# A chunk inverse on TensorE, VectorE and ScalarE, before and after its growth levels run over 32 of 64 columns

## The chip, the cores and the metric

One core of a Trainium2 chip runs the whole program in one launch. The metric is the device time of that launch in microseconds (us), the median of three runs.

## What is computed

The program is a chain of four layers on 1024 tokens of width 1024, in float32. The change lies in the second one, a RWKV-7 time mixing with 16 heads of 64. Each head carries a 64x64 state through the tokens:

```
def step(state, inp):
    r_t, w_t, k_t, v_t, al_t, be_t = inp
    sa = jnp.einsum("bhvk,bhk->bhv", state, al_t)
    state = (state * w_t[:, :, None, :] + sa[..., None] * be_t[:, :, None, :]
             + v_t[..., None] * k_t[:, :, None, :])
    return state, jnp.einsum("bhvk,bhk->bhv", state, r_t)
```

Taken in chunks of 64 tokens, the steps of a chunk are coupled by `sa`: token t needs the updates of all earlier tokens of its chunk. That coupling is a strictly triangular 64x64 matrix for each head and chunk, and all of the chunk's updates together are (identity minus that matrix) inverted, times a right side. So the kernel inverts 16 heads x 16 chunks of unit triangular 64x64 matrices.

## The kernel before

The function is `rwkv_chunks`. Two heads lie above one another on the 128 partitions (rows 0 to 63 and 64 to 127), eight such pairs `j` side by side; a group `g` is four pairs. Every 64x64 product of the stage is a float32 matmul for one head, which the trace shows as two MATMUL records and two LDWEIGHTS records; a "step" over one group is 4 pairs x 2 heads = 8 products = 16 records.

The inverse is grown block by block. `N` holds the coupling matrix, `T` the inverse so far and `Tt` its transpose. Both start as the identity (GpSimd, `start_t`); `products` on VectorE (DVE) fills the 2x2 blocks. Then for each of five levels, lv = 0 to 4, blocks of b = 2, 4, 8, 16, 32 columns are joined in twos to blocks of 2b:

- `y_step` (TensorE, L1915): Y = product of `N` (weights) and `Tt` (moving), 16 records for each group, into PSUM banks 0 and 1.
- `take_y` (ScalarE, L2077): copies Y of each group, 4 pairs x 64 columns, to SBUF.
- `z_step` (TensorE): with weights `T` and moving `Y` (L1927), and, at levels 0 to 3, with weights `Y` and moving `T` (L1931); 16 records each for each group, into banks 2 and 3.
- `grow` (DVE): two masked copies for each group, PSUM into `Tt` (L2257) and at levels 0 to 3 into `T` (L2261). The mask `tmask` lets only the new off-diagonal blocks through.

Everything is over all 64 columns, though a level's new block lies, in `Tt`, only in the second half of each 2b columns, and in `T` only in the first half.

The order of the work is written out by hand, one stream for each engine, and engines wait for each other on semaphores. For chunk c's inverse and the finish of chunk c-1 TensorE runs: first products (L1879, L1885, L1892), right sides (L1941, L1942), a bonus product (L1898), solutions (L1953), y(0), the state update (L1961, L1962), z(0), outputs of group 0, y(1), outputs of group 1 (L1968 to L1970), z(1), a turn of `b` (L1904), y(2), a turn of `v`, z(2), y(3), a turn of `k`, z(3), the variance product (L1976), y(4), z(4). So most steps of the inverse have other products between them; z(2) to y(3), and y(4) to z(4), have none. Between first products of neighbouring chunks nothing but this list stands. SyncE loads the next chunk but one (1792 KB) in the meantime.

`Y` lies in a part of an SBUF tensor that the trace calls `u`, as `N` does; so `psum<-Tt_rc,u` is y_step, `psum<-u,T_rc` is L1927 and `u<-psum` at L2077 is the copy of Y.

Of the kernel before, what the change touches and what calls it, by code (L numbers as in the profile page):

```python
# [17 lines left out]
P = 128  # L18
# [1359 lines left out]
RW_C = 64  # L1378
# [402 lines left out]
def rwkv_chunks(nc, K, A, chunk, next_round, ahead):  # L1781

    J = KT
    GJ = J // 2
    LEVELS = (1, 2, 4, 8, 16, 32)
    NL = len(LEVELS) - 1
    T_STEPS, P_STEPS = 2 * (NL + 1), 2 * NL
    with nc.cleanup_on_exit(), ExitStack() as c:
        sb = lambda n, s, d=F32: c.enter_context(nc.sbuf_tensor(f"{n}_rc", s, d))
        sem = lambda n: nc.alloc_semaphore(f"{n}_rc")  # L1790
# [4 lines left out]
        G, dist, distx, E1, E2, E3, rhs, U, N, Y, bv, hn = (spare[:, n] for n in range(12))  # L1795
# [20 lines left out]
        n_ready, ak_ready, bv_ready = sem("n_ready"), sem("ak_ready"), sem("bv_ready")  # L1816
        turned = {n: sem(f"{n}_turned") for n in "bkv"}
        taken = {n: sem(f"{n}_taken") for n in "bkv"}
        y_done, y_ready, z_done, t_ready, plain_ready = (
            sem("y_done"), sem("y_ready"), sem("z_done"), sem("t_ready"), sem("plain_ready"))  # L1820
        rhs_done, rhs_ready, u_done, u_ready = sem("rhs_done"), sem("rhs_ready"), sem("u_done"), sem("u_ready")
# [5 lines left out]
        pairs = lambda n: K.bank_pair(n).rearrange("p (j a t) -> p j a t", j=J, a=2)  # L1827
        half = lambda n, h: K.psum[:, n, h * GJ * RW_C:(h + 1) * GJ * RW_C].rearrange("p (j t) -> p j t", j=GJ)
        flat = lambda x: x.rearrange("p j t -> p (j t)")
        cols = lambda name: K.par[:, COL[name]:COL[name] + J].rearrange("p (j a) -> p j a", a=1).broadcast_to(  # L1830
            [P, J, RW_C])
        Y_BANK, Z_BANK, N_BANK, BONUS, RHS, OUT = 0, 2, 4, 5, 6, 7
# [12 lines left out]
        with nc.Block() as block:  # L1845
# [26 lines left out]
            def _(pe):  # L1872
# [35 lines left out]
                def y_step(c, q, lv):  # L1908

                    for g in range(2):  # L1910
                        pe.wait_ge(t_ready, c * T_STEPS + (2 * lv + g + 1))
                        if lv == 0 and g == 0:
                            pe.wait_ge(n_ready, c + 1)
                        for j, hp in heads(g):
                            last = pe.matmul(half(Y_BANK + g, 0)[hp, j % GJ], N[hp, j, :], Tt[hp, q, j, :],  # L1915
                                             start=True, stop=True)
                        last.then_inc(y_done, 1)

                def z_step(c, q, lv):

                    for g in range(2):
                        if lv == 0 and g == 0:
                            pe.wait_ge(ak_ready, c + 1)
                        pe.wait_ge(plain_ready, c * P_STEPS + (2 * lv + g + 1))
                        pe.wait_ge(y_ready, c * P_STEPS + (2 * lv + g + 1))
                        for j, hp in heads(g):
                            last = pe.matmul(half(Z_BANK + g, 0)[hp, j % GJ], T[hp, q, j, :], Y[hp, j, :],  # L1927
                                             start=True, stop=True)
                        if lv < NL - 1:
                            for j, hp in heads(g):  # L1930
                                last = pe.matmul(half(Z_BANK + g, 1)[hp, j % GJ], Y[hp, j, :], T[hp, q, j, :],  # L1931
                                                 start=True, stop=True)
                        last.then_inc(z_done, 1)

                def right_sides(ch, p):
# [103 lines left out]
            @block.scalar  # L2039
            def _(act):  # L2040
                act.preload_act_table_set("natural_log_exp_and_others")

                def exponentials(n, p):
                    if n > 0:
                        act.wait_ge(ar_ready, n)
                        act.wait_ge(bk_ready, n)
                    act.wait_ge(d_ready, n + 1)
                    act.activation(E2, dist, ACT.Exp, scale=RW_DECAY)
                    act.activation(E1, dist, ACT.Exp, scale=-RW_DECAY).then_inc(e12_ready, 1)
                    act.activation(E3, distx, ACT.Exp, scale=-RW_DECAY).then_inc(e3_ready, 1)  # L2050
                    act.activation(em[:, p, :], G[:, :, RW_C // 2 - 1], ACT.Exp, scale=-RW_DECAY)
                    act.activation(ee[:, p, :], dist[:, :, RW_C - 1], ACT.Exp,
                                   scale=-RW_DECAY).then_inc(em_ready, 1)

                def squares(ch):
                    act.drain()
                    act.activation(sq[:, :, :], O[:, :, :], ACT.Square).then_inc(sq_ready, 1)

                def group_rstd(ch):
                    act.wait_ge(var_done, ch + 1)  # L2060
                    act.activation(flat(rs[:, :, :]), K.psum[:, VAR, :], ACT.Ln, scale=1.0 / RW_C,
                                   bias=gn_eps[:, 0:1])
                    act.drain()
                    act.activation(rs[:, :, :], rs[:, :, :], ACT.Exp, scale=-0.5).then_inc(rs_ready, 1)

                def high_part(ch):
                    act.wait_ge(out_ready, ch + 1)
                    act.mul(K.m_hi[:, 0:J, slice(ch * RW_C, ch * RW_C + RW_C)], O[:, :, :], U_SCALE).then_inc(hi_ready, 1)

                def take(done, ready, x, b, ch):  # L2070
                    act.wait_ge(done, ch + 1)
                    act.copy(x, bank(b)).then_inc(ready, 1)

                def take_y(c, lv):
                    for g in range(2):
                        act.wait_ge(y_done, c * P_STEPS + (2 * lv + g + 1))
                        act.copy(Y[:, g * GJ:g * GJ + GJ], half(Y_BANK + g, 0)).then_inc(y_ready, 1)  # L2077

                def take_turned(c, n, x):
                    act.wait_ge(turned[n], c + 1)  # L2080
                    act.copy(x, bank(TURN[n])).then_inc(taken[n], 1)

                def body(ch, p, inverse, finish, following):
                    c, q = ch + 1, 1 - p
                    if inverse:
                        act.wait_ge(n_done, c + 1)
                        act.copy(N, bank(N_BANK)).then_inc(n_ready, 1)
                    if finish:
                        take(rhs_done, rhs_ready, rhs, RHS, ch)
                        take(u_done, u_ready, U, OUT, ch)  # L2090
                    if inverse:
                        take_y(c, 0)
                    if finish and ch > 0:
                        high_part(ch - 1)
                        act.wait_ge(lo_ready, ch)
                    if inverse:
                        take_y(c, 1)
                    if finish:
                        act.wait_ge(o_done, ch + 1)
                        act.copy(O[:, :, :], bank(OUT)).then_inc(o_ready, 1)  # L2100
                    if inverse:
                        take_turned(c, "b", bT[:, q])
                        take_y(c, 2)
                        take_turned(c, "v", vT[:, q])
                    if following:
                        exponentials(ch + 2, p)
                    if inverse:
                        take_y(c, 3)
                    if finish:
                        squares(ch)  # L2110
                    if inverse:
                        take_turned(c, "k", kT[:, q])
                        take_y(c, 4)
                    if finish:
                        group_rstd(ch)

                exponentials(0, 0)
                act.wait_ge(t_init, 1)
                chunk_steps(body)
                high_part(RW_N - 1)  # L2120
# [62 lines left out]
            def _(dve):  # L2183
# [4 lines left out]
                dve.drain()  # L2188
                dve.scalar_tensor_tensor(centre[:, :], K.pair_ones[:, :], -1.0 / RW_C, K.ident[:, :],
                                         ALU.mult, ALU.add).then_inc(centre_ready, 1)  # L2190
                dve.sem_inc(h_ready, 1)

                def summed(n, p):
# [60 lines left out]
                def grow_turned(lv, g, q, data):  # L2254

                    mask = tmask[:, 0, lv:lv + 1, :].broadcast_to([P, GJ, RW_C])
                    dve.copy_predicated(Tt[:, q, g * GJ:g * GJ + GJ], mask, data).then_inc(t_ready, 1)  # L2257

                def grow_plain(lv, g, q, data):
                    mask = tmask[:, 1, lv:lv + 1, :].broadcast_to([P, GJ, RW_C])  # L2260
                    dve.copy_predicated(T[:, q, g * GJ:g * GJ + GJ], mask, data).then_inc(plain_ready, 1)  # L2261

                def grow(c, q, lv):
                    for g in range(2):
                        dve.wait_ge(z_done, c * P_STEPS + (2 * lv + g + 1))
                        grow_turned(lv + 1, g, q, half(Z_BANK + g, 0))
                        if lv + 1 < NL:
                            grow_plain(lv + 1, g, q, half(Z_BANK + g, 1))

                def body(ch, p, inverse, finish, following):  # L2270
                    c, q, n = ch + 1, 1 - p, ch + 2
# [1106 lines left out]
```

## Time and profile before

| | |
|---|---|
| median of three runs | 3453.41 us (3447.71, 3453.41, 3459.82) |
| the profiled execution | 3451.49 us |
| its span, first to last instruction | 3449.7 us |
| PE busy (matmul records) | 3276.7 us, 95% of the span |
| DVE, ACT, POOL busy | 54%, 41%, 13% |
| mean granted TensorE clock | 0.981 |

PE is TensorE's matmul stream, PEld its weight loads, DVE is VectorE, ACT is ScalarE, POOL is GpSimd. A MATMUL record runs from its start until its result is out, so neighbouring records overlap; how fast the engine gets through them is seen from the starts, not from the durations. "Idle before, releaser" names what ended a gap; "issue" is a gap that nothing in the profile explains. The chunk stage runs from 1331 to 1850 us.

### The profile page before, as it was taken

The page shows a single profiled execution, that of the slowest core. Times are in us where ns is not written, and L with a number is a line of the kernel's source. Part 1 is how long each engine was busy: PE and PEld are TensorE (multiplying, and loading weights), DVE is VectorE, ACT ScalarE, POOL GpSimd, SP SyncE. Part 2 cuts the span into 40 slices and gives each one's busy share as a digit, 9 for nine tenths or more (in the row PEclk, how much of TensorE's full clock was granted, in tenths as well). Part 3 has the DMA queues.
Part 4 walks back from the last instruction along what each step waited for, and adds up shares of the span by engine and source line. Part 5 has one row for each costly group of instructions (what it writes and reads, how often), then busy time and mean ns, then how long its engine had stood idle before and what let it go on. Part 6 is the DMA issues. An engine that isn't in the chain of part 4 may idle for free. (4 is left out here: it accounts for less than half of the span.)

```text
span 3449.7 us, 73665 instructions
## 1 busy us (share of the span) xinstructions
PE 3276.7 (95%) x32618; PEld 2033.5 (59%) x32618; DVE 1852.2 (54%) x2557; ACT 1423.0 (41%) x2045; POOL 436.3 (13%) x302
## 2 busy tenths in 40 slices
PE   6999999999899797999999899999999999999999
PEld 3446565644444346999886466657644466657544
DVE  4666767662526524666553566654453366754342
ACT  3554545433655422333333445542322255533321
POOL 3000000020000002334331132300000232200000
PEclk9999999999999998999999999999999999999999
DMA  5111111130355552111112111021021211020211
GB/s 177 37 49 46 39 39 34 43 118 17 98 127 123 123 139 77 68 68 56 58 46 87 55 32 54 7 60 32 17 91 49 68 43 37 1 66 26 65 67 49
DMA packets 308210, 214.84 MB, mean 62 GB/s; under 512 B 125403, under 2 KB 283950, under 8 KB 305326
## 3 DMA queue, kind: packets, MB, share of 16 engines
q1 hardware_dynamic: 307464, 210.18, 20.4%
q8 instruction: 236, 3.87, 0.5%
q10 hardware_dynamic: 458, 0.37, 0.0%
q14 instruction: 52, 0.43, 0.0%
HBM read 172.74 MB, written 41.98 MB: 62 GB/s over the span
## 5 line engine op out<-in xcount | busy, mean ns | idle before, releaser
L142 PE MATMUL psum<-u,w_hi 128*128 128x512 f16 x1856 | 555.5, 381 | 17.3 <-PEq L197 5.4
L142 PE MATMUL psum<-u,w_lo 128*128 128x512 f16 x928 | 353.3, 381 | 0.0
L142 PEld LDWEIGHTS psum<-u,w_hi 128*128 128x128 f16 x1856 | 181.4, 98 | 245.8 <-issue 23.0
L115 DVE SCALAR_TENSOR_TENSOR w_lo<-stage,w_hi 128x1024 f16<-128x1024 f32 x140 | 170.4, 1238 | 217.1 <-ACT w_hi L109 216.5
L174 PE MATMUL psum<-u,w_hi 128*128 128x512 f16 x896 | 271.4, 381 | 0.0
L2650 DVE CUSTOM_DVE_ANT_0 probs_att<-psum,bias_att 128x1024 f32<-128x1024 f32 x128 | 156.8, 1225 | 165.4 <-PE psum L2445 165.0
L1071 PE MATMUL psum<-w_hi,merged 128*128 128x512 f16 x768 | 233.4, 382 | 6.8 <-PEq L3072 4.5
L2423 PE MATMUL psum<-u,w_hi 128*128 128x512 f16 x768 | 232.2, 384 | 6.7 <-PEq L1109 6.7
L1071 PE MATMUL psum<-held_hi_out,merged 128*128 128x512 f16 x768 | 231.2, 379 | 0.0
L97 POOL TENSOR_TENSOR w_hi<-stage,w_scale 128x1024 f16<-128x1024 f32 x36 | 69.1, 1920 | 946.6 <-PE psum L2423 839.3
L190 PE MATMUL psum<-w_hi,u 128*128 128x128 f16 x2048 | 173.2, 219 | 0.0
L190 PE MATMUL psum<-w_lo,u 128*128 128x128 f16 x1024 | 172.4, 219 | 0.0
L174 PE MATMUL psum<-u,w_lo 128*128 128x512 f16 x448 | 170.0, 379 | 0.0
L109 ACT ACTIVATE w_hi<-stage 128x1024 f16<-128x1024 f32 x140 | 144.7, 1050 | 55.0 <-DMA stage<-w_in 32.2
L2257 DVE COPY_PREDICATED Tt_rc<-tmask_rc,psum 128x256 f32<-128x256 uint32 x192 | 83.6, 444 | 145.1 <-PE psum L1931 121.3
L190 PEld LDWEIGHTS psum<-w_hi,u 128*128 128x128 f16 x2048 | 157.9, 98 | 4.9 <-issue 4.6
L142 PE MATMUL psum<-mix_b_rp,w_hi 128*128 128x512 f16 x480 | 145.2, 385 | 13.7 <-ACT work_rp L1681 12.7
L142 PEld LDWEIGHTS psum<-u,w_lo 128*128 128x128 f16 x928 | 91.0, 98 | 110.9 <-issue 2.1
L2559 ACT ACTIVATE probs_att<-probs_att,neg_max_att 128x1024 f32<-128x1024 f32 x128 | 146.3, 1146 | 16.2 <-DVE neg_max_att L2654 16.2
L2473 PEld LDWEIGHTS psum<-turned_att,merged 128*128 128x128 f32 x1024 | 132.6, 193 | 28.6 <-issue 14.6
L2473 PE MATMUL psum<-turned_att,merged 128*128 128x128 f32 x1024 | 138.0, 278 | 11.4 <-ACT sq_att L2573 11.0
L2423 PE MATMUL psum<-u,w_lo 128*128 128x512 f16 x384 | 147.3, 384 | 0.0
(463 smaller groups left out, 6987.6 us busy)
## 6 DMA issues: line engine op xcount, KB each, us to landing
stage<-w_in SPq DMA_DIRECT2D x72, 512.0 KB, 5.0
X<-rwkv_chunks SPq DMA_DIRECT2D x14, 1792.0 KB, 8.1
stage<-ab_w_in SPq DMA_DIRECT2D x48, 512.0 KB, 4.8
stage<-rw_w_in SPq DMA_DIRECT2D x32, 512.0 KB, 4.7
rwkv_chunks<-work_rp SPq DMA_DIRECT2D x26, 512.0 KB, 5.9
stage<-w_out SPq DMA_DIRECT2D x24, 512.0 KB, 4.2
X<-x SPq DMA_DIRECT2D x16, 512.0 KB, 8.5
stage<-ab_w_out SPq DMA_DIRECT2D x16, 512.0 KB, 4.7
```

Source lines behind the costliest of these rows:

```text
L97: pool.tensor_tensor(K.w_hi[:, slot, :], K.stage[:, slot, :], scale, ALU.mult).then_inc(K.w_half[slot], 1)
L109: act.mul(K.w_hi[:, slot, :], K.stage[:, slot, :], W_SCALE).then_inc(K.w_half[slot], 1)
L115: dve.scalar_tensor_tensor(K.w_lo[:, slot, :], K.stage[:, slot, :], W_SCALE, K.w_hi[:, slot, :], ALU.mult, ALU.subtract).then_inc(K.w_full ...
L142: last = pe.matmul(K.psum[:, bank, :], w[:, k, :], u[:, k, cols], start=(k == 0 and n == 0), stop=(k == KT - 1 and n == 2))
L174: last = pe.matmul(K.psum[:, banks[half], :], w[:, k, :], u[:, k, half * HALF:(half + 1) * HALF], start=(k == 0 and n == 0), stop=(k == KT ...
L190: last = pe.matmul(out, u[:, k, toks], w[:, k, :], start=(k == 0 and n == 0), stop=(k == KT - 1 and n == 2))
L1071: last = pe.matmul(out, m[:, 2 * u + k, t * P:(t + 1) * P], w[:, at, w_cols], start=(u == 0 and k == 0 and n == 0), stop=(u == UH - 1 and ...
L2257: dve.copy_predicated(Tt[:, q, g * GJ:g * GJ + GJ], mask, data).then_inc(t_ready, 1)
L2423: last = pe.matmul(K.psum[:, PROJ + half, :], w[:, kt, :], u[:, kt, cols(half)], start=(kt == 0 and n == 0), stop=(kt == KT - 1 and n == 2))
L2473: last = pe.matmul(K.psum[:, O_BANK, (i % 4) * P:(i % 4 + 1) * P], v_tiles[h % 2][:, half * 4 + n, :], turned[:, half, n, :], start=(half ...
L2559: act.activation(probs[:, s % 2, m, :], probs[:, s % 2, m, :], ACT.Exp, bias=neg_max[:, s % 2, m:m + 1], accum_out=sums[:, s % 2, m:m + 1] ...
L2650: dve.tensor_tensor_reduce(probs[:, s % 2, m, :], K.bank_pair(m), bias[:, h % 2, at:at + S], LOGIT_UNSCALE, LOWEST, ALU.add, ALU.max, neg_ ...
```

## The change

Two helpers choose, for level lv, the half n (0 or 1) of every 2b columns, with b = `LEVELS[lv + 1]` = 2, 4, 8, 16, 32: a view of 32 columns in runs of b. y_step and L1927 stream and write only half 1, the second product of z_step (L1931) only half 0; the copy of Y and the masked copies take the same halves. Weights stay whole (64 columns); since `Y` as weights is read whole and its other half is no longer written at level 0, `Y` is set to zero once. The number of instructions stays as it was but for that memset and its semaphore.

```diff
+        def side(x, lv, n):
+            b = LEVELS[lv + 1]
+            if len(x.shape) == 2:
+                return x.rearrange("p (n a b) -> p n a b", a=2, b=b)[:, :, n, :]
+            return x.rearrange("p j (n a b) -> p j n a b", a=2, b=b)[:, :, :, n, :]
+
+        def side_mask(n, lv):
+            b = LEVELS[lv + 1]
+            m = side(tmask[:, n, lv + 1:lv + 2, :], lv, 1 - n)
+            return m.broadcast_to([P, GJ, RW_C // (2 * b), b])
...
-                            last = pe.matmul(half(Y_BANK + g, 0)[hp, j % GJ], N[hp, j, :], Tt[hp, q, j, :],
-                                             start=True, stop=True)
+                            last = pe.matmul(side(half(Y_BANK + g, 0)[hp, j % GJ], lv, 1), N[hp, j, :],
+                                             side(Tt[hp, q, j, :], lv, 1), start=True, stop=True)
...
-                            last = pe.matmul(half(Z_BANK + g, 0)[hp, j % GJ], T[hp, q, j, :], Y[hp, j, :],
-                                             start=True, stop=True)
+                            last = pe.matmul(side(half(Z_BANK + g, 0)[hp, j % GJ], lv, 1), T[hp, q, j, :],
+                                             side(Y[hp, j, :], lv, 1), start=True, stop=True)
...
-                                last = pe.matmul(half(Z_BANK + g, 1)[hp, j % GJ], Y[hp, j, :], T[hp, q, j, :],
-                                                 start=True, stop=True)
+                                last = pe.matmul(side(half(Z_BANK + g, 1)[hp, j % GJ], lv, 0), Y[hp, j, :],
+                                                 side(T[hp, q, j, :], lv, 0), start=True, stop=True)
...
                 def take_y(c, lv):
+                    if c == 0 and lv == 0:
+                        act.wait_ge(y_zeroed, 1)
...
-                        act.copy(Y[:, g * GJ:g * GJ + GJ], half(Y_BANK + g, 0)).then_inc(y_ready, 1)
+                        act.copy(side(Y[:, g * GJ:g * GJ + GJ], lv, 1),
+                                 side(half(Y_BANK + g, 0), lv, 1)).then_inc(y_ready, 1)
...
+                dve.memset(Y, 0.0).then_inc(y_zeroed, 1)
                 dve.sem_inc(h_ready, 1)
...
-                        grow_turned(lv + 1, g, q, half(Z_BANK + g, 0))
+                        dve.copy_predicated(side(Tt[:, q, group], lv, 1), side_mask(0, lv),
+                                            side(half(Z_BANK + g, 0), lv, 1)).then_inc(t_ready, 1)
...
-                                grow_plain(lv + 1, g, q, half(Z_BANK + g, 1))
+                                dve.copy_predicated(side(T[:, q, group], lv, 0), side_mask(1, lv),
+                                                    side(half(Z_BANK + g, 1), lv, 0)).then_inc(plain_ready, 1)
```

## Rows read from the trace of the kernel before

**Rows 1.** Busy time in four stretches: length, then busy and records, clock, DMA.

```profile
core 0: us, PE busy (x) PEld busy (x) DVE busy (x) ACT busy (x) POOL busy (x), PEclk, DMA share, GB/s
1348.00:1660.00 312.00, 304.52 (x8826) 285.58 (x8823) 190.19 (x342) 112.23 (x253) 118.38 (x109) 0.99 0.18 63
```

**Rows 2.** Timeline of PE, late in a chunk: start, length from first start to last end.

```profile
1448.88 1.44 PE L1915 MATMUL psum<-Tt_rc,u 64*64 64x64 f32 x30
1450.15 1.10 PE L1904 MATMUL psum<-ident,kt_rc 64*64 64x64 f32 x32
1451.08 0.63 PE L1927 MATMUL psum<-u,T_rc 64*64 64x64 f32 x16
1451.55 0.63 PE L1931 MATMUL psum<-T_rc,u 64*64 64x64 f32 x16
...
1453.04 1.13 PE L1976 MATMUL psum<-sq_rc,pair_ones 128*128 128x512 f32 x2
1454.10 1.15 PE L1915 MATMUL psum<-Tt_rc,u 64*64 64x64 f32 x32
1455.35 1.05 PE L1927 MATMUL psum<-u,T_rc 64*64 64x64 f32 x29
```

**Rows 3.** Groups of the chunk stage on PE and PEld, shapes kept apart.

```profile
L1927 PE MATMUL psum<-u,T_rc 64*64 64x64 f32 x2560 | 114.8, 223 | 6.1 <-issue 4.2 <-ACT u L2077 0.6
L1915 PE MATMUL psum<-Tt_rc,u 64*64 64x64 f32 x2560 | 103.5, 224 | 2.2 <-issue 0.9
L1931 PE MATMUL psum<-T_rc,u 64*64 64x64 f32 x2048 | 94.0, 219 | 9.4 <-issue 9.4
L1915 PEld LDWEIGHTS psum<-Tt_rc,u 64*64 64x64 f32 x2560 | 93.0, 139 | 18.0 <-DVE Tt_rc L2257 15.0 <-issue 3.0
```

**Rows 4.** Timeline of PE, first products of another chunk.

```profile
1551.75 1.13 PE L1885 MATMUL psum<-bt_rc,ar_rc 64*64 64x64 f32 x32
1552.68 1.95 PE L1892 MATMUL psum<-ar_rc,kt_rc 64*64 64x128 f32 x32
1554.43 0.33 PE L1941 MATMUL psum<-vT_rc,ak_rc 64*64 64x64 f32 x4
```

**Rows 5.** Timeline of another stage, L716: 64 weight columns, 32 or 64 moving columns.

```profile
639.79 1.01 PEld L716 LDWEIGHTS psum<-qe_hg,ke_hg 128*64 128x64 f32 x32 [0.48 <-DVE qe_hg L954]
639.79 1.13 PE L716 MATMUL psum<-qe_hg,ke_hg 128*64 128x32 f32 x32 [0.34 <-DVE qe_hg L954]
658.92 1.02 PEld L716 LDWEIGHTS psum<-qe_hg,ke_hg 128*64 128x64 f32 x32 [0.54 <-issue]
658.93 1.15 PE L716 MATMUL psum<-qe_hg,ke_hg 128*64 128x64 f32 x32
```

**Rows 6.** Groups on DVE and ACT by shape.

```profile
L2257 DVE COPY_PREDICATED Tt_rc<-tmask_rc,psum 128x256 f32<-128x256 uint32 x192 | 83.6, 444 | 145.1 <-PE psum L1931 121.3 <-PE psum L1927 23.4
L2261 DVE COPY_PREDICATED T_rc<-tmask_rc,u 128x256 f32<-128x256 uint32 x32 | 32.5, 1067 | 3.5 <-ACT u L2087 3.5
L968 DVE COPY_PREDICATED st_hg<-room,psum 128x512 f32<-128x512 uint32 x32 | 23.3, 727 | 2.1 <-issue 2.1
L2077 ACT COPY u<-psum 128x256 f32<-128x256 f32 x160 | 59.7, 373 | 159.2 <-PE psum L1915 155.2
L2072 ACT COPY u<-psum 128x512 f32<-128x512 f32 x32 | 18.7, 585 | 72.0 <-PE psum L1942 47.3 <-PE psum L1953 24.7
```

**Rows 7.** Timelines of DVE and ACT around z(2) and y(4) of the chunk of rows 2.

```profile
1448.20 0.45 DVE L2257 COPY_PREDICATED Tt_rc<-tmask_rc,psum 128x256 f32<-128x256 uint32 x1 [1.41 <-PE psum L1931]
1448.54 0.43 DVE L2261 COPY_PREDICATED T_rc<-tmask_rc,psum 128x256 f32<-128x256 uint32 x1
1449.13 0.45 DVE L2257 COPY_PREDICATED Tt_rc<-tmask_rc,psum 128x256 f32<-128x256 uint32 x1 [0.16 <-PE psum L1931]
...
1454.83 0.84 ACT L2077 COPY u<-psum 128x256 f32<-128x256 f32 x2 [2.91 <-PE psum L1915]
```

**Rows 8.** Timelines of DVE and PE where the stage begins.

```profile
1321.29 0.48 DVE L2187 MEMSET Hs_rc<- 128x512 f32 x1
1321.86 0.29 DVE L2189 SCALAR_TENSOR_TENSOR centre_rc<-pair_ones,ident 128x128 f32<-128x128 f32 x1
1322.07 1.63 DVE L2197 TENSOR_TENSOR_SCAN u<-reset_rc,X 128x512 f32<-128x512 f32 x1
...
1331.55 3.68 PE L1879 MATMUL psum<-ar_rc,bt_rc 64*64 64x128 f32 x32 [15.56 <-DVE ar_rc L2211]
```

**Rows 9.** A pause of PE, then busy time in two stretches of 8 us.

```profile
1356.93 0.50 PE L1931 MATMUL psum<-T_rc,u 64*64 64x64 f32 x10 [2.06 <-issue]
...
1349.00:1357.00 8.00, 5.87 (x194) 5.65 (x192) 2.78 (x7) 3.66 (x9) 3.54 (x3) 1.00 0.66 231
1357.00:1365.00 8.00, 7.93 (x163) 7.79 (x164) 4.66 (x11) 1.33 (x3) 0.00 (x0) 0.79 0.02 4
```

More of the change, by code:

```diff
@@ L1818, in rwkv_chunks @@
         taken = {n: sem(f"{n}_taken") for n in "bkv"}
+        y_zeroed = sem("y_zeroed")
         y_done, y_ready, z_done, t_ready, plain_ready = (
@@ L2265, in grow @@
                         dve.wait_ge(z_done, c * P_STEPS + (2 * lv + g + 1))
-                        grow_turned(lv + 1, g, q, half(Z_BANK + g, 0))
+                        group = slice(g * GJ, g * GJ + GJ)
+                        dve.copy_predicated(side(Tt[:, q, group], lv, 1), side_mask(0, lv),
+                                            side(half(Z_BANK + g, 0), lv, 1)).then_inc(t_ready, 1)
                         if lv + 1 < NL:
-                            grow_plain(lv + 1, g, q, half(Z_BANK + g, 1))
+                            dve.copy_predicated(side(T[:, q, group], lv, 0), side_mask(1, lv),
+                                                side(half(Z_BANK + g, 1), lv, 0)).then_inc(plain_ready, 1)
                 def body(ch, p, inverse, finish, following):
```

## The prediction

> **What bounds the kernel now.** I read the busy time by stretches first, to see which engine the chunk stage leaves no room. Over 312 us of it PE is busy 304.5, DVE 190, ACT 112 [rows 1]. The busy share of a pipelined engine says little, so the timeline of PE comes next, and there the starts. A step of 32 records starts at 1450.15 and the next one at 1451.08: 0.93 us, 29.1 ns a record; 16 records take 0.47 us, the same pace [rows 2]. Nearly every step of a chunk runs at this pace, whatever its line. What departs from it is small. The last 30 records of y(3) need 1.27 us, from 1448.88 to 1450.15, where the pace gives 0.87: 0.40 beyond. z(4) starts 1.25 us after y(4), where it gives 0.93: 0.32 beyond [rows 2]. So the stage is PE's own pace, plus two waits of 0.7 us together in a chunk of 31, plus pauses without a releaser [rows 9]. The question is therefore what sets 29.1 ns, and whether 32 moving columns in place of 64 lower it.
>
> **The matmul records: y_step and z_step.** The change touches 2560 + 2560 + 2048 = 7168 records [rows 3]. Their moving columns go from 64 to 32, their weight loads stay 64x64, one for each record.
>
> What does the pace follow? With 64 weight columns and 128 moving ones, 32 records take 1.75 us, 54.7 ns each; with 64 moving ones 0.93 us, 29.1 ns [rows 4]. From 128 to 64 the moving columns set the pace. From 64 to 32 another stage of this kernel answers: it has float32 weights of 64 columns, in two tiles of the array in turn, as the two heads are here, and moves 32 or 64 columns. With 32 moving columns, 32 records last 1.13 us from first start to last end; less one record of 0.22 that is 0.91 over 31, 29.3 ns. With 64 it is 1.15, so 30 ns. The weight loads are equally far apart in both, (1.01 - 0.14)/31 = 28 ns, by a load of 0.14 [rows 5]. So the pace with 32 columns is that with 64: the loads of 64 weight columns, which the change leaves, take the place of the moving columns. I take 0 ns for each record. The difference of the two rows, 0.6 ns, times 7168 would be 4 us; I leave it in the range.
>
> The tiles there lie beside one another in columns, here above one another in rows, so the two bounds are wide. Below: if weight loads did not hold it, halving the moving columns would halve the pace as from 128 to 64, by 13 to 15 ns a record, 93 to 105 us. Above: what strided runs cost, for which no row here exists; all matmul rows of the profile that I found write contiguous columns. Per moving column the engine may become twice as slow before it shows, since 32 columns then take what 64 take. The price beyond that is a rival, below.
>
> The Trainium skill (TensorE: Matmul & The Clock Gate, section "Wait — 56ns, not 53.3ns?") puts a floor of about 25 ns between starts however few columns move. By that floor alone the sum would be an estimated 7168 x 4.1 ns = 29 us shorter, with the weight loads it is not; the rows on 32 moving columns stay above that floor [rows 5].
>
> **The masked copies (L2257, L2261).** 444 ns for 256 columns, 727 ns for 512 of the same operation with its data in PSUM [rows 6]: 1.1 ns a column, so 128 columns take about 303 ns, 141 less, if runs of 2 to 32 columns go at the same rate. Bounds: 0 less, if short runs cost twice as much each; and more than now, if the operation fell to the rate of its form with all operands in SBUF, 1067 ns for 256, thus 530 for 128, 90 more [rows 6]. I take 303, the nearest in form. DVE is not what bounds the stage, so this counts only where PE waits: at y(3). There z(2) of group 1 ends, DVE starts at 1449.13 (it was idle before, so no earlier copy delays it), and PE may go on about 0.44 later [rows 7]. The other levels have 0.9 us or more of other products between z and y. So 0.14 x 16 chunks = 2.3 us. The wait of 0.40 shrinks and does not close, so nothing else is late in its place.
>
> **The copy of Y (L2077).** 373 ns for 256 columns, 585 for 512: 0.83 a column, 267 ns for 128, 106 less [rows 6]. Bounds as above, 0 less to 106 less; a rate twice as slow for short runs gives 0. It counts at z(4), where PE waits for group 0's copy, started at 1454.83 [rows 7]. In 13 of the 16 chunks PE waits there; in the other three a delay just before hides it. 0.106 x 13 = 1.4 us. At the other levels the copy is under the state update, the outputs or a turn.
>
> **Chunk 0** has nothing of a former chunk in between, so its z(0) and y(1) wait as well: 0.1 + 0.14 = 0.25 us.
>
> **The memset of Y.** The one like it takes 0.48 us and with the step to the next instruction 0.57 [rows 8]. It stands ahead of the scan at L2197 on DVE; behind that are the distances, ACT's exponentials and `ar`, for which PE's first product waits 15.56 us [rows 8]. Nothing hides it: +0.57 us. ACT's new wait for it is met 19 us earlier than Y is first copied; nothing is held up behind it.
>
> **The sum.** -2.3 - 1.4 - 0.25 + 0.57 = -3.4 us. Against the profiled execution, 3451.5 us (span 3449.7 plus 1.8 around it), that is 3448.1. This execution lies 1.9 under the median of the runs, so for the median I put 3453.4 - 3.4 = 3450.0. What can be told from no change here is about 0.3%, 10 us; the three runs before lie 12 apart.
>
> **The rivals.**
>
> *Pace follows the moving columns.* For it: 128 to 64 did, and the tiles here are rows of the array, not columns. Against it: the weight loads alone are 28 ns apart with 32 moving columns [rows 5]. Time: 448 touched records in each of 16 chunks at 13.3 ns less are 95 us. A faster PE meets DVE and ACT earlier: z(2) of group 1 would take 0.25 us in place of 0.47, less than the two masked copies of group 0 ahead of it on DVE (0.6), so y(3) waits some 0.2 longer in each chunk, 3 us. With the 3.4 of the other terms: 3453.4 - 95 + 3 - 3 = about 3358. Half way there, 3405, also belongs here. Chance 0.11.
>
> *Strided runs slow the matmul.* The place: level 0, where the runs are 2 columns (8 bytes) with gaps of 2, and if the shape of the runs matters more, levels 1 to 3 too; at level 4 the 32 columns are contiguous. It decides from the point where a moving column costs more than twice what it costs now. If level 0's 96 records in a chunk took 58 in place of 29 ns: 96 x 16 x 29 = 45 us, 3493; if it were only a third slower, 15 us, 3463. For it the trace has nothing; against it stands the slack of two. Chance 0.12. The Trainium skill (Advanced Engine Details and Errata, section "PSUM Cachelines") speaks for it: any non-contiguous pattern slows matmuls significantly, though it asks only for every two elements in a row for best throughput, which runs of 2 still are. No row here shows either.
>
> *The pauses move.* PE stands in some chunks in the middle of z(3) with no releaser, in rows 9 for 2.06 us, while 0.66 of the DMA engines are taken, and in the stretch behind one of them the granted clock is 0.79, that is 1.2 GHz for a part of it [rows 9]. Which chunks are hit may shift with a chunk that is 0.25 us shorter. One more or less is worth 2.1 us and, at 0.21 of 8 us, 1.7 behind it: about 4 us. Two more make 3458, no change; three, 3462, or more end slower. Chance 0.07.
>
> *The forecast.* PE's pace stays, two waits shrink. Chance 0.70.
>
> **How the numbers follow.** Forecast 3450, own range 3443 to 3459, from the spread of the runs, the bounds of the copies (0 to 3.7 us of gain, or 2 us of loss) and one pause. 8 in 10 must take in the nearer parts of the rivals, so 3430 to 3466. Faster by over 0.3%: 0.11 of the first rival and 0.06 of the forecast, 0.17. Slower: 0.08 of strided runs, 0.04 of pauses, 0.02 of the forecast, 0.14. Within 0.3%: 0.69.
>
> **What would show it.** After: y and z records with 32 moving columns, still 0.47 us for 16 of them and weight loads of 0.14 at the same distances; L2257 near 303 ns, L2077 near 267; the hole in y(3) near 0.15 and z(4) 1.15 behind y(4); a chunk's period some 0.25 shorter; one more memset of 0.48 before the scan. It is wrong if 16 records of level 4 take clearly less than 0.47 us (weight loads don't hold the pace), if 16 of level 0 take clearly more (strides cost), or if the sum of the pauses changes by more than the rest.

## The result, and the profile after

| | before | after |
|---|---|---|
| median of 20 runs each | 3450.07 us (3440.65 to 3459.82) | 3467.62 us (3449.51 to 3478.62) |
| ratio, 95% interval | | 1.0053 (1.0041 to 1.0065) |
| profiled execution, its span | 3451.49, 3449.7 us | 3470.7, 3468.9 us |
| mean granted TensorE clock | 0.981 | 0.975 |
| chunk stage, first to last matmul | 525.1 us | 545.8 us |

The change makes the kernel 0.5% slower, about 18 us. The forecast was 3450 and its range ended at 3466, so it was wrong. The two profiled executions differ by 19.2 us, and the chunk stage alone by 20.7; what comes before it is about 1 us shorter. The engines after, from the first part of the profile's page:

```profile
PE 3295.3 (95%) x32618; PEld 2052.7 (59%) x32618; DVE 1812.2 (52%) x2558; ACT 1407.9 (41%) x2045; POOL 435.7 (13%) x302
```

DVE and ACT lost work (before 1852.2 and 1423.0). PE gained 18.6 us with as many records of fewer columns. The groups of the chunk stage say where (columns as in [rows 3, 6]):

```profile
L1942 PE MATMUL psum<-u,T_rc 64*64 64x32 f32 x2560 | 115.8, 224 | 9.1 <-issue 7.8 <-ACT u L2094 1.4
L1930 PE MATMUL psum<-Tt_rc,u 64*64 64x32 f32 x2560 | 102.7, 225 | 1.4 <-issue 1.4
L1946 PE MATMUL psum<-T_rc,u 64*64 64x32 f32 x2048 | 95.2, 221 | 8.2 <-issue 8.2
L2286 DVE COPY_PREDICATED Tt_rc<-tmask_rc,psum 128x128 f32<-128x128 uint32 x160 | 52.3, 327 | 183.9 <-PE psum L1946 144.5 <-PE psum L1942 39.4
L1894 PE MATMUL psum<-ar_rc,bt_rc 64*64 64x128 f32 x512 | 45.1, 345 | 15.6 <-DVE ar_rc L2230 15.6
...
L2094 ACT COPY u<-psum 128x128 f32<-128x128 f32 x160 | 42.9, 269 | 175.2 <-PE psum L1930 171.1
```

L1942, L1930 and L1946 are the narrowed products; their means are within 2 ns of those of [rows 3]. The line that grew is one that the change does not touch. L1894 is the first products, L1879 before, where its row was:

```profile
L1879 PE MATMUL psum<-ar_rc,bt_rc 64*64 64x128 f32 x512 | 33.4, 282 | 15.6 <-DVE ar_rc L2211 15.6
```

It went from 282 to 345 ns. In each chunk these products come right behind z(4). An undisturbed chunk does what the forecast said. PE's timeline late in such a chunk after the change, the stretch of [rows 2] one chunk on:

```profile
1490.34 1.26 PE L1930 MATMUL psum<-Tt_rc,u 64*64 64x32 f32 x30
1491.44 1.13 PE L1919 MATMUL psum<-ident,kt_rc 64*64 64x64 f32 x32
1492.40 0.61 PE L1942 MATMUL psum<-u,T_rc 64*64 64x32 f32 x16
1492.84 0.63 PE L1946 MATMUL psum<-T_rc,u 64*64 64x32 f32 x16
...
1495.39 1.12 PE L1930 MATMUL psum<-Tt_rc,u 64*64 64x32 f32 x32
1496.50 1.12 PE L1942 MATMUL psum<-u,T_rc 64*64 64x32 f32 x32
```

The starts of the two steps shown are 0.44 us apart, against 0.47 before; the pairs behind them stay at 0.47. y(3) lasts 1.10 from start to start where it took 1.27, z(4) starts 1.11 behind y(4) where it took 1.25 [rows 2]. The chunk's period falls from 30.95 to 30.61 us.

The loss lies behind the pauses. A pause is here a gap of over 1.2 us between the starts of neighbouring records of PE. One after the change, in z(3) of another chunk, on PE's timeline, and the busy time (columns as in [rows 1]) in stretches cut along it:

```profile
1424.34 0.63 PE L1946 MATMUL psum<-T_rc,u 64*64 64x32 f32 x16
1427.45 0.95 PE L1942 MATMUL psum<-u,T_rc 64*64 64x32 f32 x16 [2.48 <-issue]
...
1429.18 2.07 PE L1991 MATMUL psum<-sq_rc,pair_ones 128*128 128x512 f32 x2
1431.19 1.92 PE L1930 MATMUL psum<-Tt_rc,u 64*64 64x32 f32 x32
1432.92 1.90 PE L1942 MATMUL psum<-u,T_rc 64*64 64x32 f32 x32
1434.62 3.52 PE L1894 MATMUL psum<-ar_rc,bt_rc 64*64 64x128 f32 x32
1437.98 1.09 PE L1900 MATMUL psum<-bt_rc,ar_rc 64*64 64x64 f32 x32
...
1424.00:1428.00 4.00, 1.52 (x49) 1.44 (x45) 0.49 (x2) 0.70 (x2) 0.48 (x1) 0.95 0.61 255
1428.00:1431.00 3.00, 3.00 (x26) 1.62 (x23) 1.69 (x4) 0.00 (x0) 0.00 (x0) 0.50 0.02 5
1431.00:1434.60 3.60, 3.60 (x65) 3.41 (x66) 0.30 (x1) 1.64 (x4) 0.00 (x0) 0.50 0.00 0
1434.60:1437.80 3.20, 3.20 (x35) 3.20 (x34) 0.99 (x2) 0.11 (x1) 1.63 (x2) 0.50 0.02 5
1437.80:1440.00 2.20, 2.20 (x58) 2.20 (x56) 1.64 (x4) 0.59 (x1) 1.94 (x2) 0.98 0.00 0
```

The granted clock is 0.50 (1.2 GHz) from the end of the pause to the last of the first products (L1894), 10.2 us. The 32 first products take 3.36 us from start to start; before, behind such a pause, they took 1.75. Here is one of those, from the timeline and the busy time of the kernel before:

```profile
1742.39 0.45 PE L1927 MATMUL psum<-u,T_rc 64*64 64x64 f32 x9 [2.00 <-issue]
...
1743.24 1.57 PE L1976 MATMUL psum<-sq_rc,pair_ones 128*128 128x512 f32 x2
1744.74 1.98 PE L1915 MATMUL psum<-Tt_rc,u 64*64 64x64 f32 x32
1746.50 1.46 PE L1927 MATMUL psum<-u,T_rc 64*64 64x64 f32 x32
1747.76 1.95 PE L1879 MATMUL psum<-ar_rc,bt_rc 64*64 64x128 f32 x32
1749.51 1.13 PE L1885 MATMUL psum<-bt_rc,ar_rc 64*64 64x64 f32 x32
...
1743.80:1747.20 3.40, 3.40 (x48) 2.46 (x48) 1.52 (x4) 0.81 (x3) 0.00 (x0) 0.50 0.00 0
1747.20:1754.00 6.80, 6.80 (x183) 6.80 (x180) 5.68 (x9) 1.74 (x3) 3.59 (x3) 1.00 0.01 2
```

A like pause, with the same steps behind it, but the clock is back after 3.4 us, while z(4) runs. Over the stage there were six pauses (14.5 us together) before and five stretches at 1.2 GHz of 3.4 us, 17.0 us. After, there were eight pauses (17.6 us), of which seven last 2.0 to 2.7 us and one 1.2; behind the seven lie one low stretch of 6.8 us and six of 10.2, 68.0 us. The low clock at the start of the stage, which ends during chunk 0's first products in all runs, is left out of these sums. The 51 us more at half the clock are worth up to 25.5 us. With 3.1 us more of pauses, and 16 x 0.34 = 5.4 less by shorter waits, that makes up to 23; the stage grew by 20.7. The other executions agree: the mean granted clock is 0.973 to 0.978 in all 20 of the kernel after, and 0.979 to 0.986 in the 29 of the kernel before that ran beside the first four experiments.

### The profile page after: what moved, and what is told of

It reads as the page before. It is cut to its first block and busy times, and to the rows that moved or that the text cites. A ratio compares the mean times of both kernels' runs of the same rounds, so it can differ in the third digit from the quotient of the medians.

```text
span 3468.9 us, 73667 instructions
## 1 busy us (share of the span) xinstructions
PE 3295.3 (95%) x32618; PEld 2052.7 (59%) x32618; DVE 1812.2 (52%) x2558; ACT 1407.9 (41%) x2045; POOL 435.7 (13%) x302
## 5 line engine op out<-in xcount | busy, mean ns | idle before, releaser
L2495 PEld LDWEIGHTS psum<-turned_att,merged 128*128 128x128 f32 x1024 | 131.7, 191 | 28.6 <-issue 14.5
L2286 DVE COPY_PREDICATED Tt_rc<-tmask_rc,psum 128x128 f32<-128x128 uint32 x160 | 52.3, 327 | 183.9 <-PE psum L1946 144.5
```

What stands on the lines that cost most here:

```text
L2286: dve.copy_predicated(side(Tt[:, q, group], lv, 1), side_mask(0, lv), side(half(Z_BANK + g, 0), lv, 1)).then_inc(t_ready, 1)
L2495: last = pe.matmul(K.psum[:, O_BANK, (i % 4) * P:(i % 4 + 1) * P], v_tiles[h % 2][:, half * 4 + n, :], turned[:, half, n, :], start=(half ...
```

## The experiments

The ratio is always that to the kernel before, run in the same batch. "Low" is the time at 1.2 GHz within the stage in the one profiled execution, that at the start of the stage left out.

**Matmuls alone.** The change, with the copy of Y and both masked copies over 64 columns again.

```diff
-                        act.copy(side(Y[:, g * GJ:g * GJ + GJ], lv, 1),
-                                 side(half(Y_BANK + g, 0), lv, 1)).then_inc(y_ready, 1)
+                        act.copy(Y[:, g * GJ:g * GJ + GJ], half(Y_BANK + g, 0)).then_inc(y_ready, 1)
...
+                        grow_turned(lv + 1, g, q, half(Z_BANK + g, 0))
...
+                            grow_plain(lv + 1, g, q, half(Z_BANK + g, 1))
```

> Only the matmuls run over 32 columns; the copy of Y and the masked copies are those of before, over 64. Theory A: the loss comes from the 32-column products alone, through the clock: after a pause in z(3) the clock stays at 1.2 GHz some 10 us in place of 3.4, so seven chunks of 35 to 38 us, L1894 (first products) at a mean near 345 ns in place of 282; without the 0.25 us a chunk that the copies give back, 1.006 to 1.008 of before (3471 to 3478). Rival B: the narrower copies shift the stages and so the pauses; then this kernel is before's time, 3450, within 5. Rival C: strides cost TensorE time: then 16 records take over 0.47 us at level 0.

3473.05 against 3447.62 us, ratio 1.0066 (1.0047 to 1.0085). Low 71.4 us. Of this, 6.8 us lie in chunk 0 and 3.4 in a later chunk, with no pause over 1.2 us before them. The whole loss is there without any shorter copy, so the rival that the copies shift something falls. Behind the pause at 1724 the busy time shows the clock as after the change:

```profile
1728.00:1737.00 9.00, 9.00 (x128) 8.18 (x128) 3.50 (x8) 1.96 (x4) 2.90 (x3) 0.52 0.01 2
1737.00:1739.00 2.00, 2.00 (x47) 2.00 (x45) 1.12 (x4) 0.59 (x1) 0.68 (x1) 1.00 0.00 0
```

**Copies alone.** The other half: matmuls over 64 columns, copies over 32.

```diff
-                            last = pe.matmul(side(half(Y_BANK + g, 0)[hp, j % GJ], lv, 1), N[hp, j, :],
-                                             side(Tt[hp, q, j, :], lv, 1), start=True, stop=True)
+                            last = pe.matmul(half(Y_BANK + g, 0)[hp, j % GJ], N[hp, j, :], Tt[hp, q, j, :],
+                                             start=True, stop=True)
```

And so for both products of z_step.

> Only the copy of Y and the masked copies run over 32 columns; the matmuls are those of before. Theory A: the gain that the prediction summed, 3 to 6 us, and low stretches as short as before: 0.9985, near 3446. Rival B (the shift of the stages is what costs): near 3467, 1.005.

3445.64 us, 0.9997 (0.9985 to 1.0008). Low 17.0 us, as before. The profiled stage is 3.3 us shorter, but the gain does not stand out of the spread of the runs.

**The last level wide.** The change, with y(4) and z(4) over 64 columns; levels 0 to 3 stay narrow.

```diff
+                            if lv < NL - 1:
                                 last = pe.matmul(side(half(Y_BANK + g, 0)[hp, j % GJ], lv, 1), N[hp, j, :],
                                                  side(Tt[hp, q, j, :], lv, 1), start=True, stop=True)
+                            else:
+                                last = pe.matmul(half(Y_BANK + g, 0)[hp, j % GJ], N[hp, j, :], Tt[hp, q, j, :],
+                                                 start=True, stop=True)
...
```

> The kernel after, but y(4) and z(4), the products that run behind the pause and the variance product, are over 64 columns again; levels 0 to 3 stay at 32. Theory A: those two steps are what TensorE does when the clock is low, so it comes back as soon as before: 3445 to 3450, 0.999. Rival D (the columns of all levels count, because the clock falls by what went before): 3460 to 3468, long low stretches.

3446.53 us, 0.9992 (0.9981 to 1.0004): the loss is gone. The pauses are not gone: eight, 19.1 us. Six of the seven low stretches are 3.4 us long, one 6.8, in all 27.2. Busy time behind one pause, cut where the clock comes back:

```profile
1424.00:1427.40 3.40, 3.40 (x56) 2.87 (x56) 1.10 (x2) 1.11 (x3) 0.00 (x0) 0.52 0.00 0
1427.40:1434.00 6.60, 6.60 (x173) 6.60 (x171) 5.36 (x9) 1.23 (x3) 3.59 (x3) 0.99 0.01 2
```

So whether these 64 records a chunk, between the pause and the first products, move 32 or 64 columns decides most of the length.

**The last level alone narrow.** The kernel before, with only the matmuls of y(4) and z(4) over 32 columns (the condition of the last diff turned round, all copies wide).

> The kernel before (all copies over 64 columns), but the matmuls of y(4) and z(4) over 32. Theory A: nearly the whole loss comes back with a third of the narrow products gone: 1.004 to 1.007, long low stretches (L1894-like first products near 340 ns in the mean). Rival D: 0 to a third of it, 3450 to 3457.

3457.74 us, 1.0024 (1.0010 to 1.0039), low 47.7 us. This is a loss, but under the bound expected. In the profiled execution the low stretches are 6.8, 10.2, 3.4, 10.2, 3.4 and 13.7 us: behind some pauses the clock returns early even with narrow y(4) and z(4). That execution took 3467.12 us, close to the slowest of the twelve, so a usual one probably has less low clock; the mean granted clock of the twelve runs from 0.976 to 0.984. The last level is needed for the loss; that it suffices for all of it is not shown. What the narrow products of the other levels add is left open.

**No burst of DMA.** The pauses fall together with SyncE's load of the next chunk but one (1792 KB in one DMA, 0.61 of the DMA engines in the stretch above). Here each load brings 32 KB; the chunk stage's inputs are left out but for these. Once with the kernel before, once with the change.

```diff
-                    sp.dma_start(raw[:, p], A["scratch"][ch]
-                                 ).then_inc(raw_in[p], 16)
+                    sp.dma_start(raw[:, p, G_, 0:1], A["scratch"][ch, :, G_, 0:1]).then_inc(raw_in[p], 16)
```

> The kernel before, but each of the 14 loads of a chunk's inputs (1792 KB) brings only one pair's gate, 32 KB; the rest of the chunk's inputs stays that of the first two chunks, so the output leaves this out. If the pauses of TensorE in z(3) come with the load, none over 1.2 us is left and no low clock after the first products of chunk 0: 14.5 us of pauses, 8.5 of low clock and the small delays go, some 25 to 28 us: 3420 to 3425, 0.9925. If they come from elsewhere: 3447.

> The same edit on the kernel after (the same inputs left out). Theory A: with no pause there is no low clock to stay in, and what the prediction summed is left: 3 to 6 us less than the kernel before with small loads, so 3416 to 3421, 0.991 of before; periods of a chunk 30.6 us throughout. Rival E (narrow products are slower to run at this place in themselves, or lower the clock without a pause): 15 us or more over before with small loads, near 3440.

Before so: 3429.20 against 3448.45, 0.9938 (0.9922 to 0.9955), a little above the 3420 to 3425 expected. After so: 3420.61, 0.9920 (0.9901 to 0.9938). Neither profiled execution has a pause or a low stretch, and the order of the two turns round: the narrow kernel's median is 8.6 us the lower. The intervals overlap; in the profiled executions the stage takes 495.5 us against 500.4, 4.9 less, within the 3 to 6 expected. Busy time over the stretch of [rows 1], first the narrow one, then the wide one:

```profile
1348.00:1660.00 312.00, 312.00 (x9236) 295.45 (x9232) 177.45 (x356) 109.02 (x269) 120.85 (x111) 1.00 0.02 5
```

```profile
1348.00:1660.00 312.00, 310.21 (x9112) 291.78 (x9110) 195.14 (x352) 117.07 (x265) 120.48 (x110) 1.00 0.02 5
```

124 records more in 312 us without a change of clock: that is the gain of the change by itself.

**The load in pieces.** The whole load, as seven DMAs of 256 KB, each behind a step of the former chunk.

```diff
-            eng.wait_ge(raw_in[p], ch * 8 + (16 - 8 * p))
+            eng.wait_ge(raw_in[p], (ch - p) * 8 * RW_ARRAYS + 16)
...
-                    sp.dma_start(raw[:, p], A["scratch"][ch]
-                                 ).then_inc(raw_in[p], 16)
+                    for a in range(RW_ARRAYS):
+                        if a:
+                            sem_, count = ((turned["k"], ch - 1), (z_done, (ch - 1) * P_STEPS), (ab_done, ch),
+                                           (n_done, ch), (ak_done, ch), (bonus_done, ch))[a - 1]
+                            sp.wait_ge(sem_, count)
+                        sp.dma_start(raw[:, p, a], A["scratch"][ch, :, a]).then_inc(raw_in[p], 16)
```

> The kernel before, all inputs loaded, but the load in seven pieces of 256 KB, each behind a later step of TensorE (turn of v, turn of k, z(4), the first products, the bonus). If the pauses come from the whole load in one burst, they shrink below 1 us: 3425 to 3435, 0.995. If any load of this kind stalls TensorE, it has more and shorter pauses and stays at 3447.

> The split load on the kernel after. Theory A: without the long pauses the narrow products cost nothing: 3420 to 3432, 3 to 6 us less than before with the split load. Rival E: 15 us more than that.

Before so: 3429.15, 0.9940 (0.9921 to 0.9959). After so: 3428.88, 0.9936 (0.9918 to 0.9953). No pause in either, and in the stretch of [rows 1] the share of the DMA engines is even higher than before:

```profile
1348.00:1660.00 312.00, 310.21 (x9098) 291.58 (x9095) 195.00 (x352) 116.76 (x265) 120.05 (x110) 1.00 0.23 64
```

So the pauses go with the burst, not with the bytes. The trace also has what the burst holds up. The queue q1 carries the loads. The queue q8 brings instructions in packets of 16 KB; the median distance between two is 128 matmul records of PE, so they are taken here for TensorE's. DMA queues of the kernel before, from 1348.7 to 1354.5 us, during a load and ahead of the pause of [rows 9] (packets, MB, share of the 16 engines):

```profile
q1 hardware_dynamic: 100, 1.43, 73.2%
```

and with the load in pieces, over the same 5.8 us:

```profile
q1 hardware_dynamic: 276, 0.50, 26.2%
q8 instruction: 2, 0.03, 2.0%
```

In the kernel before no such packet starts for 7.4 us, from 1347.23 to 1354.59; the usual distance is 4.0. The late packet starts behind PE's 564th matmul record of the stage, and the same packet behind the 466th with the split load and the 452nd with the small load. It is in at 1355.52, and PE goes on at 1356.93. All 14 pauses of the kernels before and after look like this: 207 to 245 records lie between the starts of two packets, where no two lie over 178 apart in the four kernels with small or split loads above, and PE goes on 1.3 to 1.6 us behind the end of the second. The reading that fits is that TensorE runs out of instructions because the burst delays their packets. That the packets are late is shown. That nothing else holds TensorE is argued from these times, since no run delays the packets alone.

But the two differ by 0.3 us, where 3 to 6 were expected. In the profiled execution the narrow one has one low stretch of 6.8 us in chunk 0, where nothing of a former chunk lies between the levels. Busy time there, narrow:

```profile
1344.00:1352.00 8.00, 7.93 (x165) 7.91 (x166) 3.67 (x9) 1.65 (x5) 3.99 (x4) 0.57 0.01 2
```

and wide:

```profile
1344.00:1352.00 8.00, 7.93 (x271) 7.79 (x268) 4.79 (x10) 4.86 (x12) 4.81 (x5) 1.00 0.12 37
```

Its first chunk takes 28.7 us where the wide one takes 25.2. That is 3.5 of the missing gain, and it happened without a pause. The kernel with the matmuls alone narrow and the pace probe below have the same stretch at 1344 us; of the seven kernels with narrow matmuls at levels 0 to 3 these three have it, of the others none.

**Two ways to keep the gain.** The split load with the last level wide, and the split load with the copies alone narrow.

> The kernel after with y(4) and z(4) over 64 columns and the load in seven pieces. In the run of the kernel after with split loads the one low stretch left was 6.8 us in chunk 0. If the width of the last level decides there too, it goes or gets shorter: 3422 to 3426, 0.993; if chunk 0's narrow levels 0 to 3 hold the clock down, as in the kernel after with split loads: 3429.

> All matmuls over 64 columns, the copies over 32, the load in seven pieces: the gain of the copies (0.34 us a chunk by the periods 30.95 and 30.61) without any narrow product. No low clock behind chunk 0's first products: 3422 to 3426, 0.993 of before, 4 to 6 us below the kernel before with split loads (3429). If the 32-column products themselves brought part of that 0.34, it is 3427.

3425.08 against 3447.51, 0.9939 (0.9923 to 0.9955), and 3425.57, 0.9934 (0.9918 to 0.9950). No pause and no low stretch in either, chunk 0 included. The intervals do not tell them apart from the split load alone.

**What sets the pace.** In the kernel after, y(4) over 16 moving columns with 64 weight columns, and z(4) over 32 moving with 32 weight columns. Part of the last level's blocks is left out.

```diff
+                                last = pe.matmul(half(Y_BANK + g, 0)[hp, j % GJ, 48:64], N[hp, j, :],
+                                                 Tt[hp, q, j, 48:64], start=True, stop=True)
...
+                                top = slice(hp.start, hp.start + 32)
+                                last = pe.matmul(half(Z_BANK + g, 0)[top, j % GJ, 32:64], T[hp, q, j, 0:32],
+                                                 Y[hp, j, 32:64], start=True, stop=True)
```

> A look at what sets the pace. The kernel after, but y(4) moves and writes 16 columns in place of 32, and z(4) loads 32 weight columns in place of 64 and moves 32 (so part of the last level's blocks is left out). If the loads of 64 weight columns set the pace, 16 records of y(4) still take 0.47 us and 16 of z(4) clearly less, 0.25 to 0.35. If a floor for each record does, both stay at 0.47. If moving columns did, y(4) would be shorter.

PE's timeline in a chunk at full clock:

```profile
1498.43 1.11 PE L1931 MATMUL psum<-Tt_rc,u 64*64 64x16 f32 x32
1499.53 0.91 PE L1948 MATMUL psum<-u,T_rc 64*32 64x32 f32 x32
```

With 16 moving columns y(4) lasts what it lasts with 32 (1.12). In z(4) the 16 records of group 0 all start within 0.25 us, 15.5 ns each: with 32 weight columns the pace doubles. The 0.91 holds a wait between the groups. So the number of weight columns sets the pace here.

**The block that is really new.** At the last level only a 32x32 corner of each product is needed. Split load, copies over 32 columns, levels 0 to 3 with wide matmuls, y(4) and z(4) with 32 weight and 32 moving columns.

```diff
+                                top = slice(hp.start, hp.start + 32)
+                                last = pe.matmul(half(Y_BANK + g, 0)[top, j % GJ, 32:64], N[hp, j, 0:32],
+                                                 Tt[hp, q, j, 32:64], start=True, stop=True)
...
+                                last = pe.matmul(half(Z_BANK + g, 0)[top, j % GJ, 32:64], T[hp, q, j, 0:32],
+                                                 Y[hp, j, 32:64], start=True, stop=True)
```

> The kernel with narrow copies and the load in seven pieces, and y(4) and z(4) over 32 weight columns and 32 moving ones: at the last level only rows 0 to 31 and columns 32 to 63 of each head are new, so the result is whole. Levels 0 to 3 stay at 64 columns on TensorE. If the loads of the weight columns set the pace (16 records in 0.25 us in the look before), y(4) and z(4) together go from about 2.04 us to 1.3, with a wait for the copy of Y between them: 0.7 us in each of 16 chunks, 11 us: 3414, 0.990 of before. If the wait eats it: 3425. If the narrow steps bring back low clock: over 3430.

3417.00 against 3445.59, 0.9921 (0.9905 to 0.9936): the fastest kernel here that does the whole work, 29 us under the kernel before in its batch. Its interval still overlaps those of the other kernels with split loads. PE's timeline:

```profile
1505.39 0.70 PE L1936 MATMUL psum<-Tt_rc,u 64*32 64x32 f32 x32
1506.30 0.69 PE L1953 MATMUL psum<-u,T_rc 64*32 64x32 f32 x32 [0.20 <-ACT u L2108]
1506.92 1.31 PE L1898 MATMUL psum<-ar_rc,bt_rc 64*64 64x128 f32 x20
```

y(4) and z(4) take 1.53 us together, of which z(4) waits 0.20 for the copy of Y. A chunk's period is 30.17 us, where it is 30.69 with the split load and the narrow copies alone: 0.52 shorter; 0.7 were expected.

## Why the prediction was wrong

**PE's pace stays: right.** 0 ns a record was taken, and 16 records of 64x32 take 0.44 to 0.47 us at every level. The reason given, the 64 weight columns, is shown by the pace probe. With it the rival "pace follows the moving columns" (3358) falls.

**Strided runs: right.** Level 0, with runs of two columns, after the change:

```profile
1478.12 0.65 PE L1942 MATMUL psum<-u,T_rc 64*64 64x32 f32 x16
1478.56 0.68 PE L1946 MATMUL psum<-T_rc,u 64*64 64x32 f32 x16
1479.03 0.68 PE L1942 MATMUL psum<-u,T_rc 64*64 64x32 f32 x16
```

The starts are 0.44 and 0.47 us apart, as at level 3 in the timeline of the result. A slower pace for strides does not show under the weight loads. The Trainium skill (Advanced Engine Details and Errata, section "PSUM Cachelines") has any non-contiguous pattern slow matmuls significantly; for these patterns the trace disagrees, and its half-sentence on two consecutive elements is what fits.

**The copies: right in size and place.** 303 ns was taken for the masked copy, 267 for the copy of Y, which took 269. DVE's timeline, level 0 and level 2:

```profile
1479.28 0.45 DVE L2286 COPY_PREDICATED Tt_rc<-tmask_rc,psum 128x128 f32<-128x128 uint32 x1 [1.06 <-PE psum L1946]
...
1489.66 0.30 DVE L2286 COPY_PREDICATED Tt_rc<-tmask_rc,psum 128x128 f32<-128x128 uint32 x1 [1.69 <-PE psum L1946]
```

0.30 us holds at levels 1 to 4. At level 0 the runs of two cost as much as the whole 64 did, the bound of "0 less"; the path does not run there but in chunk 0. y(3) and z(4) gave 0.17 and 0.14 us a chunk, against 0.14 and 0.106 x 13/16 forecast, and the period 0.34 where 0.25 was forecast. Not all of it is the copies': with the copies alone narrow the period is 30.69 us, 0.26 shorter, and z(4) starts 1.14 behind y(4). The other 0.08 us a chunk come with the narrow products, for which the sum had 0; in 16 chunks that is 1.3 us.

**The memset: too dear.** It takes its 0.48 us, but the scan behind it then takes less:

```profile
1320.71 0.29 DVE L2207 SCALAR_TENSOR_TENSOR centre_rc<-pair_ones,ident 128x128 f32<-128x128 f32 x1
1321.05 0.48 DVE L2209 MEMSET u<- 128x512 f32 x1
1321.46 1.16 DVE L2216 TENSOR_TENSOR_SCAN u<-reset_rc,X 128x512 f32<-128x512 f32 x1
```

From the start of `centre_rc` to the scan's end it is 1.91 us against 1.84 [rows 8]; 0.57 was taken, 0.07 is measured.

**The pauses move: the step that failed.** The forecast priced a pause at 2.1 us and the low clock behind it at 1.7, "at 0.21 of 8 us", from the kernel before [rows 9], and asked only whether pauses would shift. Their number rose by two, within what it allowed; the 3.1 us more that they take is the small part of the loss. What changed was the term it held fixed: the low clock lasts 6.8 to 10.2 us in place of 3.4 behind the pauses that were there already, so it costs up to 5 us each and not 1.7: 51 us more at half the clock, up to 25.5 us that the sum had at nothing. It hung on what PE does after the pause, which is just what the change edits: the products behind z(3) are narrow. That PE's pace does not depend on the number of columns was true at full clock, and it was taken for all that the columns could do. Matmuls alone (1.0066) and the last level wide (0.9992) show the cause from both sides; the small loads show the rest of the forecast by itself: a stage 4.9 us shorter, where the sum had 4.0 for it; the memset lies ahead of the stage's first product.

The rival's sign and place were right. Its chance of 0.07 was too small, because its price left out that the low clock behind a pause can grow.

**Open.** Why the last level alone gives only part of the loss. Why chunk 0's clock falls without a pause in three kernels with narrow products and not in the other four. And whether the late instruction packets are all that holds TensorE during the burst.

## What to carry to other kernels

Where the weight loads set the pace, fewer moving columns save next to nothing; fewer weight columns do. A change that makes records smaller at an equal pace is not neutral where pauses occur: look at the granted clock behind each pause in the kernel before, and ask what the work there will be after the change. A pause without a releaser beside a large load is worth a look at the instruction packets in the DMA queues, and an experiment with the load in pieces, before anything on the engine is tuned; here that was worth 0.6%, more than any edit of the inverse.

## What the runs showed of the hardware

- Behind a pause of 2 to 3 us the clock was 1.2 GHz mostly for 3.4 us where y(4) and z(4) move 64 columns (once for 6.8, once not at all), and mostly for 6.8 to 10.2 us where they move 32, with the same number of records and weight loads. In the low stretch of the change y(4) took 1.73 us from start to start, at full clock 1.11, a wait included.
- float32 products in two row tiles in turn: 29 ns a record with 64 weight columns, for 16, 32 and 64 moving columns alike, and 15.5 ns with 32 weight columns.
- Runs of two float32 columns cost a masked copy on DVE 0.45 us for 128 elements in each partition, longer runs 0.30; on matmuls with 64 weight columns no cost shows (16 records in 0.44 to 0.47 us).
- A load of 1792 KB in one DMA goes with pauses of TensorE's stream of 1.2 to 3.8 us; as seven of 256 KB, spread over the chunk, with none.
- Ahead of each of the 14 pauses in the kernels before and after, 207 to 245 matmul records lay between the starts of two 16 KB instruction packets, where 128 is usual, and PE went on 1.3 to 1.6 us behind the end of the late one.
